# HGRN2 mixer of a two-layer decoder: values and decayed keys turned by VectorE's 32x32 blocks and a DRAM scratch instead of TensorE

## What is computed

```python
def step(s, inp):                      # one chunk of tokens
    qc, kc, vc, gc = inp
    cum = jnp.cumsum(gc, axis=2)
    o_inter = jnp.einsum('bhtk,bhkv->bhtv', qc * jnp.exp(cum), s)
    decay = jnp.exp(jnp.where(causal, cum[:, :, :, None, :] - cum[:, :, None, :, :], -jnp.inf))
    att = jnp.einsum('bhtk,bhsk,bhtsk->bhts', qc, kc, decay)
    o = o_inter + jnp.einsum('bhts,bhsv->bhtv', att, vc)
    last = cum[:, :, -1:, :]
    s_new = jnp.exp(last[:, :, 0, :])[..., None] * s + jnp.einsum(
        'bhsk,bhsv->bhkv', kc * jnp.exp(last - cum), vc)
    return s_new, o
```

## Time and profile before

| | |
|---|---|
| median of 3 runs | 1516.17 us |
| the profiled execution | 1516.44 us, its span in the trace 1514.6 us |
| TensorE busy | 1479.3 us (98%) |
| VectorE / ScalarE / GpSimd busy | 991.3 (65%) / 678.2 (45%) / 419.9 us (28%) |
| chain that ended last | TensorE 84%, VectorE 6%, ScalarE 5%, DMA 2% |
| DMA | mean 198 GB/s; SyncE's queue 56.8% of 16 engines' time |
| first mixer, steady heads | one head every 68.15 us |

### The profile page before, as it was taken

One profiled execution on the slowest core, in us unless ns is written; L12 is line 12 of the kernel. 1 busy time (PEld: TensorE's weight loads), 2 busy tenths in 40 slices (PEclk: granted clock), 3 DMA queues, 4 the chain that ended last, 5 costly groups with the idle time before them and its releaser, 6 DMA issues.

```text
span 1514.6 us, 23379 instructions
## 1 busy us (share of the span) xinstructions
PE 1479.3 (98%) x8437; PEld 1090.5 (72%) x8437; DVE 991.3 (65%) x1987; ACT 678.2 (45%) x1380; POOL 419.9 (28%) x335
## 2 busy tenths in 40 slices
PE   7999999999999999999999999999999999989998
PEld 6888888888888875446777777777777777754443
DVE  6868696877868684126377677758677676748321
ACT  4445545444445552212356555546555455545100
POOL 5012322121212101012051625443452615332200
PEclk9999999999999999999999999999999999999999
DMA  9683938466483943323247779596968778698731
GB/s 268 192 240 97 292 105 260 147 190 200 150 239 99 299 155 108 102 64 128 61 124 197 251 217 305 178 279 210 280 215 248 260 229 294 185 324 315 238 134 58
DMA packets 290505, 300.53 MB, mean 198 GB/s; under 512 B 25863, under 2 KB 247295, under 8 KB 290391
## 3 DMA queue, kind: packets, MB, share of 16 engines
q1 hardware_dynamic: 279254, 262.44, 56.8%
q0 software_dynamic: 11136, 36.59, 7.1%
HBM read 243.57 MB, written 122.53 MB: 242 GB/s over the span
## 4 chain that ended last, share of the span: by engine, by line
PE 84%; DVE 6%; ACT 5%; DMA 2%; issue 2%; SPq 1%; POOL 0%; DVEq 0%; POOLq 0%
PE psum L2134 42%; PE psum L2158 7%; PE psum L2646 7%; PE psum L2446 4%; PE psum L2472 4%; PE psum L2211 3%; PE psum L2097 2%; PE psum L2504 2%; PE psum L2406 2%; ACT psum L1274 1%; ACT psum L1283 1%; PE psum L2281 1%; PE psum L2222 1%; PE psum L2297 1%; PE psum L2299 1%
## 5 line engine op out<-in xcount | busy, mean ns | idle before, releaser
L2134 PE MATMUL psum<-arena 128*128 128x252 f32 (+1 forms) x3472 | 811.4, 384 | 2.2 <-DVE arena L1451 2.2
L2134 PEld LDWEIGHTS psum<-arena 128*128 128x128 f32 x3472 | 640.8, 190 | 124.0 <-issue 23.1
L949 POOL TENSOR_TENSOR arena<-arena 128x1024 f32<-128x1024 f32 x64 | 158.2, 2472 | 374.2 <-DMA arena<-k_pages 368.8
L1451 DVE TENSOR_TENSOR arena<-arena,psum 128x252 f32<-128x252 f32 (+1 forms) x310 | 128.8, 416 | 160.5 <-PE psum L2134 155.7
L2646 PE MATMUL psum<-arena 128*128 128x512 f32 x256 | 115.6, 604 | 4.5 <-DMA arena<-o_heads 2.9
L2158 PE MATMUL psum<-arena 128*128 128x512 f32 x256 | 113.0, 594 | 0.1
L1024 ACT COPY arena<-psum 128x252 f32<-128x252 f32 (+1 forms) x124 | 46.2, 373 | 139.5 <-PE psum L2134 139.4
L2646 PEld LDWEIGHTS psum<-arena 128*128 128x128 f32 x256 | 47.6, 192 | 63.2 <-issue 60.7
L2158 PEld LDWEIGHTS psum<-arena 128*128 128x128 f32 x256 | 47.5, 190 | 57.4 <-issue 56.5
L1087 ACT ACTIVATE arena<-arena 128x1024 f32<-128x1024 f32 x48 | 50.7, 1056 | 84.6 <-DVE arena L1497 84.2
L1274 ACT ACTIVATE psum<-psum,arena 128x640 f32<-128x640 f32 (+3 forms) x64 | 58.9, 921 | 59.9 <-DVE arena L1798 59.9
(11 more groups left out here) (272 smaller groups left out, 2086.4 us busy)
## 6 DMA issues: line engine op xcount, KB each, us to landing
k_pages<-in_cache_k SPq DMA_DIRECT2D x64, 512.0 KB, 6.5
v_pages<-in_cache_v SPq DMA_DIRECT2D x64, 512.0 KB, 7.2
arena<-k_pages SPq DMA_DIRECT2D x64, 512.0 KB, 5.3
arena<-v_pages SPq DMA_DIRECT2D x64, 512.0 KB, 6.8
arena<-in_w_in_a SPq DMA_DIRECT2D x32, 512.0 KB, 6.9
arena<-in_x_prompt SPq DMA_DIRECT2D x16, 512.0 KB, 7.5
arena<-in_w_kv SPq DMA_DIRECT2D x16, 512.0 KB, 6.6
arena<-in_w_in_b SPq DMA_DIRECT2D x16, 512.0 KB, 7.6
```

What stands on the lines that cost most here:

```text
L949: pool.tensor_tensor(k_ring[:, m % 2], k_ring[:, m % 2], q_all[:, m % S:m % S + 1, :].broadcast_to([P, PAGES, P]), ALU.mult).then_inc(kq_m ...
L1451: dve.tensor_tensor(out, more, bank[n % 2][:, 0:size(u)], ALU.add).then_inc(of.by_dve, 1)
L2134: ins = pe.matmul(bank[n % 2][:, 0:size(u)], w[:, k, :], x[:, k, :], start=(k == 0 and r in (0, 1, 3, 4)), stop=(k == HK - 1), skip_group_ ...
```

## The change

Per head, TensorE's 16 transposes and ScalarE's 4 copies of them go. VectorE turns `raw_v` and `k_dec` in 32x32 blocks (`turn_tokens`, one instruction each over 128 x 1024). SyncE stores the blocks to a DRAM scratch, four stores of 128 KB for a set (`tokens_out`), and loads them back whole, 512 KB (`tokens_in`). In the loaded layout the 128 columns of a block of tokens are four groups of 32, 256 words apart. So where v or k is the stationary operand, each product becomes four, one for each 32 columns, which fill 32 partitions of the bank each: the updates go from 8 products to 32, the products of `v_tok` with `att` from 8 to 32. The 7 products with `s_all` stay, but come after all of the 32 and not between them. `exp_kd` moves before `exp4`, `k_dec` and its turning before the sample adds; TensorE's updates move from after `fq(7)` to after `fq(9)`, behind a new wait for the load. `fq(8)` on VectorE goes ahead of `chunk_states(0)`. `sort_pages` is cut in halves: the second half of head h+1 follows the token loads, the first half of h+2 follows the reload of the norm strips; three halves instead of two are issued at the start. In the last head SyncE stores and reloads the tokens behind the loads for the output projection. `k_dec` lies in `t1` instead of `logf`.

```diff
+        v_blocks = area(T)
+        v_tok = v_blocks.rearrange("p (g t l) -> p t g l", g=4, l=32)
...
+        k_blocks = o_rs[:, 0:T]
+        k_dec_tok = k_blocks.rearrange("p (g t l) -> p t g l", g=4, l=32)
...
-        def sort_pages(sp, s):
-
-            for j in range(PAGES):
+        def sort_pages(sp, s, half):
+
+            for j in range(HALF * half, HALF * half + HALF):
...
-            sort_pages(sp, 0)
+            for s, half in ((0, 0), (0, 1), (1, 0)):
+                sort_pages(sp, s, half)
+
+            def tokens_out(h, n, blocks):
+
+                sp.wait_ge(blocks_turned, 2 * token_set(h, n))
+                if h:
+                    sp.wait_ge(pt_moved, MOVES * token_set(h - 1, n))
+                dst = token_rows[n].rearrange("(r l) (g n) -> g l r n", r=4, g=4)
+                for g in range(4):
+                    src = blocks[32 * g:32 * g + 32].rearrange("p (r n) -> p r n", r=4)
+                    sp.dma_start(dst[g], src).then_inc(rows_stored, 16)
+
+            def tokens_in(h, n, blocks):
+                sp.wait_ge(rows_stored, STORES * token_set(h, TOKEN_SETS - 1 if h == AH - 1 else n))
+                sp.dma_start(blocks, token_rows[n]).then_inc(pt_moved, 16)
...
+            for h in range(AH):
+                if h == AH - 1:
+                    sp.wait_ge(o_stored, 16 * (AH - 2))
+                    sp.wait_ge(vecs.sem, vecs.at("q", AH - 1))
+                    for n in range(EARLY):
+                        sp.dma_start(o_heads[n], o_dram[n]).then_inc(early_loaded, 16)
+                if h < AH - 1:
+                    tokens_out(h, 0, v_blocks)
+                sp.wait_ge(units.done, vg_unit(h, 14))
+                if h + 2 < AH:
+                    load_w(sp, h // 2 + 1, h % 2)
+                elif h + 2 == AH:
+                    sp.dma_start(w_o[:, 0:AH // 2], w_o_rows[:, 0:AH // 2]).then_inc(w_o_loaded, 16)
+                else:
+                    for n in range(EARLY, AH - 2):
+                        sp.dma_start(o_heads[n], o_dram[n]).then_inc(o_loaded, 16)
+                    sp.dma_start(w_o[:, AH // 2:AH], w_o_rows[:, AH // 2:AH]).then_inc(w_o_loaded, 16)
+                    res_in(0)
+                    res_in(1)
+                    tokens_out(h, 0, v_blocks)
+                if h < AH - 1:
+                    tokens_in(h, 0, v_blocks)
+                    tokens_out(h, 1, k_blocks)
+                else:
+                    tokens_out(h, 1, k_blocks)
+                    tokens_in(h, 0, v_blocks)
+                tokens_in(h, 1, k_blocks)
+                if h < AH - 1:
+                    sort_pages(sp, h + 1, 1)
+                    sp.wait_ge(o_strips_set, h + 1)
+                    if h:
+                        sp.wait_ge(o_rs_loaded, 16 * h)
+                    sp.dma_start(o_rs_row.rearrange("(j s n) -> s j n", j=2, n=P),
+                                 o_rs[0:P:32, 0:T].rearrange("p (j m) -> p j m", j=2)[:, :, 0:P]).then_inc(o_strips_stored, 16)
+                    sp.wait_ge(o_strips_stored, 16 * (h + 1))
+                    sp.dma_start(o_rs[:, 0:T], o_rs_row.partition_broadcast(P)).then_inc(o_rs_loaded, 16)
+                    if h + 2 < AH:
+                        sort_pages(sp, h + 2, 0)
...
                 level(16)
                 vg(9)
                 level(8)
+                for t in range(NC):
+                    end = t * P if t >= NC // 2 else t * P + C - 1
+                    ins = act.activation(t1[:, cols(t)], cum[:, cols(t)], ACT.Exp, bias=cum[:, end:end + 1], scale=-1.0)
+                ins.then_inc(acts.sem, 1)
                 level(4)
                 level(2)
-                for j in range(2):
-                    act.wait_ge(uu_done.sem, uu_done.at(f"v_turn{j}", h))
-                    act.copy(v_tok[:, 4 * j:4 * j + 4, :], bank[4 + j][:, :]).then_inc(uu_taken_a, 1)
...
+                def turn_tokens(n, out, src):
+
+                    dve.transpose(out.rearrange("p (r t l) -> p t r l", r=4, l=32),
+                                  src.rearrange("p (t r l) -> p t r l", r=4, l=32)).then_inc(blocks_turned, 2)
...
+                dve.wait_ge(*units.taken(vg_unit(h, 9)))
+                dve.wait_ge(*units.taken(vg_unit(h, 12)))
+                turn_tokens(0, v_blocks, raw_v[:, 0:T])
...
                 factors(2)
                 fq(1)
                 merge(4)
+                a("exp_kd")
+                dve.tensor_tensor(k_dec, k_h[:, 0:T], t1[:, 0:T], ALU.mult).then_inc(vecs.sem, 1)
+                dve.wait_ge(vecs.sem, vecs.at("k_dec", h))
+                turn_tokens(1, k_blocks, k_dec)
                 a("s_kept")
                 for j in range(2):
                     dve.wait_ge(uu_done.sem, uu_done.at(f"outer{j}", h))
                 factors(1)
                 merge(2)
                 fq(4)
-                a("exp_kd")
-                dve.tensor_tensor(k_dec, k_h[:, 0:T], t1[:, 0:T], ALU.mult).then_inc(vecs.sem, 1)
                 merge(1)
                 fq(5)
                 a("ln_g")
                                 bank[6][:, 2 * P:4 * P].rearrange("p (y g n) -> p y g n", y=2, n=32)[:, :, :, 31]).then_inc(vecs.sem, 1)
                 dve.tensor_tensor(q_dec, q_dec, q_h[:, 0:T], ALU.mult).then_inc(vecs.sem, 1)
                 dve.wait_ge(s_all_free, h + 1)
+                fq(8)
                 chunk_states(0)
-                fq(8)
                 chunk_states(1)
...
-                for j in range(2):
-                    pe.wait_ge(uu_taken_v, 4 * h + 3 + j)
-                    for t in range(4 * j, 4 * j + 4):
-                        ins = pe.transpose(bank[4 + j][:, t % 4 * P:(t % 4 + 1) * P], raw_v[:, cols(t)], ident)
-                    ins.then_inc(uu_done.sem, 1)
                 fq(0, 1)
                 level(4)
                 v("v_diag")
-                pe.wait_ge(uu_taken_a, 4 * h + 2)
                 for r in range(2):
                     rows = slice(UPPER * r, UPPER * (r + 1))
+                    pe.wait_ge(uu_taken_v, 4 * h + 3 + r)
                     pe.matmul(bank[4 + r], k_smp[rows, :], v_diag[rows], start=True, stop=True).then_inc(uu_done.sem, 1)
                 fq(2, 3)
                 level(2)
                 fq(4)
                 level(1)
                 fq(5)
-                v("k_dec")
-                for j in range(2):
-                    pe.wait_ge(uu_taken_v, 4 * h + 5 + j)
-                    for t in range(4 * j, 4 * j + 4):
-                        ins = pe.transpose(bank[4 + j][:, t % 4 * P:(t % 4 + 1) * P], k_dec[:, cols(t)], ident)
-                    ins.then_inc(uu_done.sem, 1)
                 for b in range(S):
                     g = 32 * (b % 4)
                     ins = pe.matmul(bank[6][g:g + 32, b // 4 * P:b // 4 * P + P], q_h[:, T + b - 31:T + b + 1], s_smp[:, b, :],
...
                     ins = pe.transpose(bank[6][:, (2 + y) * P:(3 + y) * P], o_row[:, y * P:y * P + P], ident)
                 ins.then_inc(smp_done.sem, 1)
                 fq(7)
-                pe.wait_ge(uu_taken_a, 4 * h + 4)
-                for j in range(2):
-                    for c in range(4 * j, 4 * j + 4):
-                        ins = pe.matmul(bank[4 + j][:, c % 4 * P:(c % 4 + 1) * P], k_dec_tok[:, block_of(c), :], v_tok[:, block_of(c), :],
-                                        start=True, stop=True)
-                    ins.then_inc(uu_done.sem, 1)
                 pe.wait_ge(acts.sem, acts.at("sq_smp", h))
                 pe.matmul(bank[6][:, 16:16 + S], ones_mean, sq_smp, start=True, stop=True)\
                   .then_inc(smp_done.sem, 1)
-                fq(8, 9, 10)
+                fq(8, 9)
+                pe.wait_ge(pt_moved, MOVES * token_set(h, 1))
+                for j in range(2):
+                    pe.wait_ge(uu_taken_v, 4 * h + 5 + j)
+                    for c in range(4 * j, 4 * j + 4):
+                        for g in range(4):
+                            ins = pe.matmul(bank[4 + j][32 * g:32 * g + 32, c % 4 * P:(c % 4 + 1) * P], k_dec_tok[:, block_of(c), g],
+                                            v_tok[:, block_of(c)], start=True, stop=True, skip_group_check=True)
+                    ins.then_inc(uu_done.sem, 1)
+                fq(10)
                 if h + 1 < AH:
                     fq(11, 12, 13)
                 v("q_dec")
                 pe.wait_ge(lv_taken_v, 9 * h + 9)
                 pe.wait_ge(uu_taken_v, 4 * h + 8)
                 pe.wait_ge(acts.sem, acts.at("ln_smp", h))
+                order = [2 * (t % 4) + t // 4 for t in range(TT)]
                 for t in range(TT):
-                    dst = bank[6 + t // 4][:, t % 4 * P:(t % 4 + 1) * P]
-                    c = 2 * (t % 4) + t // 4
-                    ins = pe.matmul(dst, v_tok[:, t, :], att[:, cols(t)], start=True, stop=(c == 0), skip_group_check=True)
-                    if c:
```

(8 more changed lines are left out.)

53 lines of the change are left out of this document (12 added, 41 removed).

## The result

The change makes the kernel slower by a little: 1519.27 us (median of 7 runs, 1517.82 to 1524.11) against 1516.17 for the kernel before beside it (7 runs, 1514.46 to 1517.72), a ratio of 1.0028 with a 95% interval of 1.0019 to 1.0037. By the medians that is +3.1 us, by the ratio +4.2. The forecast was 1508.5. The profiled execution took 1518.31, with a span of 1516.5; the kernel before had 1516.44 and 1514.6.

The account below looks back on a forecast made before the run. TensorE was taken to bound the first mixer's steady head, busy 68.15 of 68.15 us. Seven heads at -1.46 (-10.2) and the last at +2.6 made -7.6: 1508.5 us against the median, range 1503 to 1521.

Parts of the forecast that it names:

- what leaves its stream shortens the head one for one: Steady head of the first mixer: TensorE never waits, busy 68.15 of 68.15 us, so work removed from it shortens the head equally.
- The reordering of updates and units moves no work in or out.: TensorE's stream in a steady head: placing the updates later was counted as neither adding nor removing time.
- The stream, -1.46 a head: TensorE per steady head: transposes gone -1.89, narrow updates +0.22, narrow outputs +0.21; bounds -1.89 and -0.89 us.
- VectorE's margin, 0.3 us: Middle of head: with turnings at 1.19 us each, factors(1) ends at 434.1, 0.3 us before TensorE reaches level(1) at 434.4.
- The first rival: VectorE late at level(1) because turnings cost 2.4 us beside GpSimd: 1514.8, or 1523 with both; chance 0.14.
- The tokens' trip: Keys through DRAM, before the updates: 11 us taken (7.2 to 14.5), landing about 443, 2 us early in a 13.2 us window.
- The second rival: Keys land late and TensorE stands at the updates: 1.3 us in seven heads, 3.7 in the last, 1521; chance 0.20.
- The last head, +2.6: Last head: outputs start 2.4 us later, waiting for VectorE's second half of the states (1.49 us), plus 0.2 for the outputs.
- The rivals: Late VectorE 0.14; late keys 0.20; narrow products one after another, about 1600, 0.03; last head and small excesses larger, 1514, 0.05.
- the chance of 0.62 for faster: Whole kernel under 1513.1 us: 0.58 from the forecast and 0.04 from a milder form of the first rival.

Follow-up runs that it names:

- experiment 1: GpSimd's F and Q weight sums left out in heads 1 to 6: in the changed kernel 1515.18 us, in the kernel before 1516.88 us.
- experiment 5: Changed kernel with GpSimd's F and Q sums right after the prompt state's store is issued: 1512.34 us; second kernel also has weights behind the token loads: 1512.21 us.
- experiment 8: Updates moved back behind unit 7: in the changed kernel 1548.79 us; second kernel, the same in experiment 5's kernel with weights last, 1511.32 us.
- experiment 3: Kernel before with only its updates and outputs split into four column groups, transposes staying on TensorE: 1520.61 us, ratio 1.0028.
- experiment 4: Changed kernel with the updates of the last head alone put ahead of part(8): 1518.67 us, ratio 1.0011 to the kernel before.

## Why the prediction was wrong

Point by point, by its own steps:

- **TensorE is busy 68.15 of 68.15 us, so "what leaves its stream shortens the head one for one".** This is the step that failed. The prediction checked two margins, VectorE's in the middle of the head and the trip's, and no margin at the head's start, where VectorE's first steps wait for the stream that was to get shorter. There 0.3 us of reserve was left at most: heads that could be 67.05 came to 67.5 to 68.4, the start of GpSimd's first sum plus 13.96 each. Its own and the earlier trace rows showed the mechanism (1.40 instead of 0.68 beside GpSimd), but it was applied to the turnings, which it doesn't touch, and not to the operations with two SBUF sources whose place beside GpSimd moves. Worth 6.0 us of the 10.8 that the forecast missed (shown by experiments 1 and 5).
- **"The reordering of updates and units moves no work in or out."** Nearly true of TensorE: with the updates back behind unit 7 (experiment 8, the second kernel) the heads are 66.94 instead of 67.05, so the new order costs 0.11. And not enough: the prediction followed the later update to `chunk_states` and stopped before the state's store and GpSimd's sums behind it. The update's 2.2 us reach the store as 0.4 only, but a shorter head needed the sums earlier, at about 53.1 behind the mark by that distance, and they stayed at 53.5 to 54.4.
- **The stream, -1.46 a head.** Mechanism right, size off: -1.10, inside its bounds of -1.89 to -0.89. The narrow groups cost 0.59 instead of 0.43 (experiment 3), and the rest gives back 1.69, not 1.89. Of that last 0.20 the updates' new place takes 0.11; where the other 0.09 stays, no row shows. 2.5 us in seven heads.
- **VectorE's margin, 0.3 us.** Nearly right, 0.15 left: `turn_tokens` 1.23 and 1.25 against 1.19, `factors(1)` from 433.59 to 434.26 against a computed 433.5 to 434.1, no wait at 434.41. The first rival didn't happen.
- **The tokens' trip: the keys land at 443, 2 us early.** The price was too low: 13.1 us from the turning's end (432.2) to the landing (445.3), not 11, and the reserve nothing instead of 2. The 2 MB of weights ahead of it are the reason for 5.4 us of it (13.3 against 7.9 in the two kernels of experiment 5). In the profiled execution next to no wait came of it; in others it did (experiments 1 and 4), and the kernel after scatters over 6.3 us where the one before has 3.3. What that scatter is made of is not shown for this kernel; in the one long execution looked at (experiment 4) it was more the sums' start than the trip. The second rival was near: with 3.6 us less of cover it is what happens (experiment 8).
- **The last head, +2.6.** Right down to the updates: relative to the head's mark they start at 583.3 where 583.4 was worked out. Then two terms were off. The prediction let the second half of the states, 1.49 us, start when the updates end. But the whole chain is 0.29 + 2.65 us (L1564, L1566 x7) and starts only when the first half of the updates is done, at 582.72, so its second half starts 0.7 behind the end of the updates: the outputs start 3.1 later than before, not 2.4. And the lower clock, 1.5, was in no step. Sum +5.0.
- **The rivals.** None of the four named VectorE at the head's start or a clock that falls behind a wait. The time, 1519.3, lies within the range, on the side of the late trip and for another reason; the chance of 0.62 for faster rested on the step that failed.

Put right, the sum is 7 x (-1.10) + 6.0 + 5.0 = +3.3, and 3.1 was measured (4.2 by the ratio).

## What to carry to other kernels

An engine that is busy all the time bounds a loop only up to the reserve of whatever stands next; before its time is counted as gain, ask at every point where it takes up another engine's result how early that result is, above all at the loop's start, where the others wait for it in turn. Look above all for what does not move when the stream gets shorter: here GpSimd's sums, which start behind a store's landing, and beside which VectorE's operations with two SBUF sources ended 1.1 us behind GpSimd's. And an edit that pays in a steady loop can cost much of it again in the last pass (5.0 of 7.7 us), where its cover is missing: there the old way, kept for one pass, was worth 3.8 us here (1512.21 to 1508.42; 3.0 by the last head's length).

## What the runs showed of the hardware

- VectorE and GpSimd took turns: a `logf` of 1.23 us with two SBUF sources took up to 3.27, a scan of 1.22 took 2.18 to 2.23, and each ended 1.1 us behind the end of a GpSimd instruction in the four cases looked at; GpSimd's sums took up to 2.15 instead of 1.28 in these cases. A block transpose of 128 x 1024 with one source was untouched, at 1.24.
- 32 products (64 records) with 32 columns each in four groups, 128 columns moving, took 1.88 to 1.89 us from start to start against 1.78 for 8 wide ones, and two such sets lengthened a head by 0.59.
- The granted clock went to 0.50 and 0.53 for 2 to 3 us behind idle stretches of TensorE of 1.95, 2.46 and 3.11 us, and stayed at 1.00 behind one of 2.43 us in the same place of another kernel (experiment 5); behind one of 1.92 the products took their 1.96 as well, and in experiment 1's last head it stayed at 1.00 at first behind one of 2.43 and was at 0.50 two microseconds later. What tells these apart was not settled.
- 512 KB stored to DRAM and read back took 13.1 us from turning to landing with 2 MB of weights issued ahead of them, and 7.9 with the weights behind; the load was issued 7.8 and 3.8 us behind the first store.
